# Memory stage in three token passes, with routing in short pieces, in a hybrid sparse/forgetting-attention and expert-retrieval step

## The chip, the cores and the metric

The kernel runs on one core of one Trainium2 chip. The metric is the time of one launch on the device in microseconds (us), the median of several runs. Engines: TensorE (PE), VectorE (DVE), ScalarE (ACT), GpSimd (POOL) and SyncE (SP), whose queue only issues DMA transfers. ScalarE and GpSimd can issue transfers too; the indirect ones (gathers of rows by index) are issued by GpSimd.

## The reference, cut to what matters

One layer over 1024 prompt tokens and 32 sample tokens, width 1024, in float32. After attention:

```python
h = x + concat([o_a, o_f]) @ w_out
h = h + memory_attention(rms_norm(h, g_mem), w_q, mk, mv, w_o)   # 4 heads of 256, 256 memory tokens
h = h + peer_ffn(rms_norm(h, g_ffn), ...)

def peer_ffn(xb):                       # per token, 8 heads
    q = xb @ w_q                        # 2048 wide: two halves of 128 per head
    s1, s2 = q[..., :half] @ keys1.T, q[..., half:] @ keys2.T      # 128 scores each
    v1, i1 = top_k(s1, 16); v2, i2 = top_k(s2, 16)
    sv, si = top_k(v1[:, None] + v2[None, :], 16)                  # of 256 pairs
    e = i1 * 128 + i2 at si             # expert numbers, of 16384
    return sum(softmax(sv) * gelu(xb . u[e]) * v[e])
```

## The kernel before, in words

Activations lie transposed: 128 partitions, 8 slices of the width (KD), tokens along the free axis. Tokens are in nine tiles: eight of 128 prompt tokens and one of the 32 sample tokens. Five of them (tiles 0 to 3 and the sample's, NSP = 544 tokens) are **gathered**: for each of their experts the rows of u and v are fetched by index. For 544 columns of indices that are 544 indirect transfers of 128 rows of 4 KB from u, each followed by one **dot** on VectorE (L1813, `dot`), a product with the token's own row, summed along 1024. Four prompt tiles (ND = 512 tokens) are **dense**: the hidden values of all 16384 experts are computed with matmuls (128 chunks of 128 experts, `DenseHidden`) and weighted later by spread gates.

A product in float32 precision is made of three fp32r products: weights and activations are each split in a high part (rounded) and a low part (the difference), and high x high, high x low and low x high are added. A **weight block** is 128 output rows by 1024: one load of 512 KB into one of two buffers `w`, a cast to the high part (L972) and a subtraction for the low part (L974), both on GpSimd (`split_w`), then 8 x 3 matmuls (L995, `product`) into one of three PSUM banks. `split_w` waits until the product two blocks back is done; a load waits for the split two blocks back.

A **pass** (`Mixer`) runs 40 blocks over its tokens: MIX 0 to 7 (output projection, added to h by `add_out`), a norm, QRY 8 to 15 (memory queries, `scale_q`), memory attention in units of one head and one token tile (`attend`, `attend_act`, `attend_dve`), ATT 16 to 23 (its output projection, added to h), a norm, PKQ 24 to 39 (the expert queries, copied by ScalarE, stored to the scratch tensor s_pq). Pass 1 is `sparse_mixer`: 544 tokens in two spans of 272 columns, so each block has 48 matmuls; 20 attention units; between MIX and QRY it also computes memory keys and values. It ends with a barrier, since it is a block of its own. Pass 2 is the first part of `route`: 512 tokens, 24 matmuls of 512 columns per block, 16 units.

**Routing** of one tile (its scores from s_pq and the keys on TensorE, then 20 ordered steps on VectorE: top-16 of each half by MAX8 and MATCH_REPLACE8, the 64 candidate pairs, top-16 again, the decoding of the positions by one-hot products of 2048 columns, L1970 to L1987) is written for VectorE as one list per tile, j = 0 to 8 in the order 0, 1, 2, 3, sample, 4 to 7. Between the ordered steps `beside` puts other work at fixed places: for j = 0 the adds of MIX (`OUT_AFTER`), for j = 1 the QRY scalings, the whole memory attention with three dots per unit, dots and the adds of ATT; for j >= 2 four dots after each of 16 steps. So pass 2 has tiles 0 and 1 in it by hand, and tile 2 begins after them. GpSimd issues the gathers in its own order between the splits, four row buffers up to dot 68 and twelve after it; a gather waits for the dot that last used its buffer.

**The hidden stage** is the second part of `route`: for chunk n ScalarE rounds the u block (L1472) and applies gelu to the product (L1495), GpSimd subtracts (L1477) and issues gathers (L1759), TensorE multiplies (L1487), SP loads and stores. The chunks are dealt to tiles by `CHUNKS_AT`; at the last chunk of group j ScalarE waits for tile j-1's scores to be sorted (`exponents(j - 1)`) before it goes on. After it come the gates (`spread_gates`) and the second half (`experts`).

## Time and profile before

| what | value |
|---|---|
| time, median of 3 runs (lowest to highest) | 4199.35 us (4198.51 to 4213.7) |
| the profiled execution: time, span | 4206.49 us, 4204.7 us |
| mean granted TensorE clock | 0.926 |
| busy: PE, DVE, ACT, POOL | 3559.5, 2489.5, 997.3, 2022.3 us |
| attention | 0 to 988 us |
| pass 1 | 988 to 1420 us |
| pass 2 | 1420 to 1887.8 us |
| hidden stage | 1887.8 to 2797 us |
| gates and second half | 2797 to 4204.7 us |

Times in a profile are counted from the span's start. The granted clock is a share of full speed: 1.00 is 2.4 GHz and 0.50 is 1.2 GHz, and a value between is a mean over a stretch that had both. The end of a matmul is modelled and successive ones overlap, so the pace is read from the starts. The bracket behind a timeline row is the idle time of the engine before it, and what ended that.

### The profile page before, as it was taken

Reading aid. Unit: us, or ns where it says so; the run is one execution under the profiler, and the core shown is the slowest. Engines: PE = TensorE matmul, PEld = TensorE weight load, DVE = VectorE, ACT = ScalarE, POOL = GpSimd, SP = SyncE. Lnnn points to the kernel's source line nnn. Section 1 sums busy time; section 2 is a strip of 40 time slices with the busy share of each in tenths; the row PEclk is TensorE's granted clock in tenths of the full one; section 3 lists DMA queues with packets and bytes.
Section 4 is the critical chain, followed back from the end, with each engine's and each line's share of the span. In section 5 each row is a group of like instructions: output and inputs, shape, how many; then the busy total and the mean of one; then the engine's idle time right before and its main releaser. Section 6 shows DMA issues by size and latency. Waiting matters only on the chain. (4 is left out here: it accounts for less than half of the span.)

```text
span 4204.7 us, 50892 instructions
## 1 busy us (share of the span) xinstructions
PE 3559.5 (85%) x17397; PEld 2546.1 (61%) x17413; DVE 2489.5 (59%) x5829; ACT 997.3 (24%) x1843; POOL 2022.3 (48%) x1518
## 2 busy tenths in 40 slices
PE   7888888897978874789898888957769999999996
PEld 4445566566768763567676666645535556566554
DVE  3878884332222375877999999998723333233333
ACT  1213333242121111113222222223212122122121
POOL 0000000003114443687888888855457677777762
PEclk9888998898999996899999999989979999999998
DMA  2011000003303435599999999969999999999983
GB/s 105 13 35 31 17 7 11 10 0 137 105 21 113 147 110 180 185 330 334 365 396 363 380 385 363 386 244 358 354 333 345 358 352 345 351 364 363 362 334 142
DMA packets 370010, 960.31 MB, mean 228 GB/s; under 512 B 33680, under 2 KB 119576, under 8 KB 368256
## 3 DMA queue, kind: packets, MB, share of 16 engines
q0 software_dynamic: 156672, 570.49, 35.7%
q1 hardware_dynamic: 205280, 363.30, 24.8%
q10 hardware_dynamic: 7840, 23.74, 1.5%
q8 instruction: 121, 1.98, 0.2%
q14 instruction: 97, 0.79, 0.1%
HBM read 862.73 MB, written 94.68 MB: 228 GB/s over the span
## 5 line engine op out<-in xcount | busy, mean ns | idle before, releaser
L1487 PE MATMUL m_ps<-m_xh,m_wh 128*128 128x512 f32 x3072 | 766.0, 407 | 100.1 <-POOL m_wh L1477 100.1
L2334 PE MATMUL e_y_ps<-e_wh,e_vh 128*128 128x512 f32 x3072 | 742.5, 398 | 51.0 <-DVE e_wh L2452 43.1
L1487 PEld LDWEIGHTS m_ps<-m_xh,m_wh 128*128 128x128 f32 x3072 | 585.2, 194 | 274.7 <-POOL m_wh L1477 142.3
L2334 PEld LDWEIGHTS e_y_ps<-e_wh,e_vh 128*128 128x128 f32 x3072 | 570.5, 189 | 269.7 <-issue 116.4
L972 POOL CAST m_wh<-m_w 128x1024 fp32r<-128x1024 f32 x80 | 84.6, 1057 | 1342.1 <-DMA m_w<-in_w_out 988.5
L995 PE MATMUL m_ps<-m_xh,m_wh 128*128 128x272 f32 (+1 forms) x2880 | 502.0, 335 | 65.6 <-DVE m_xh L1053 20.1
L995 PEld LDWEIGHTS m_ps<-m_xh,m_wh 128*128 128x128 f32 x2880 | 436.9, 194 | 127.4 <-issue 41.4
L2043 POOL DMA_INDIRECT e_rows<-in_v,idt x448 | 437.8, 977 | 119.7 <-issue 106.9
L2487 DVE TENSOR_TENSOR oT<-e_y_ps,oT 128x512 f32<-128x512 f32 x256 | 175.4, 685 | 520.6 <-PE e_y_ps L2334 520.6
L2412 POOL TENSOR_TENSOR e_vh<-e_v,e_vh 128x1024 fp32r<-128x1024 f32 x128 | 306.7, 2397 | 239.8 <-ACT e_vh L2357 238.5
L2076 PE MATMUL z_ps<-e_rows,flat 128*32 128x512 f32 x1792 | 291.5, 609 | 45.8 <-DMA e_rows<-in_v,idt 45.6
L1477 POOL TENSOR_TENSOR m_wh<-m_w,m_wh 128x1024 fp32r<-128x1024 f32 x128 | 313.1, 2446 | 13.8 <-ACT m_wh L1472 11.6
L1759 POOL DMA_INDIRECT oT<-in_u,eid x224 | 228.2, 1019 | 144.3 <-DVE hn L1813 108.0
L1813 DVE CUSTOM_DVE_ANT_0 oT<-oT,m_row_ps 128x1024 f32<-128x1024 f32 x224 | 262.6, 1212 | 29.5 <-DMA oT<-in_u,eid 28.5
L2365 ACT ACTIVATE e_wh<-e_hid 128x512 fp32r<-128x512 f32 x128 | 80.7, 632 | 746.0 <-DVE e_hid L2447 739.0
L2447 DVE TENSOR_TENSOR e_hid<-e_hid,e_gate 128x512 f32<-128x512 f32 x128 | 114.1, 892 | 208.9 <-DMA e_gate<-s_gate 208.9
L1495 ACT ACTIVATE flat<-m_ps 128x512 f32<-128x512 f32 x128 | 76.6, 598 | 597.0 <-PE m_ps L1487 596.9
L1813 DVE CUSTOM_DVE_ANT_0 m_q<-m_q,m_row_ps 128x1024 f32<-128x1024 f32 x160 | 188.0, 1211 | 33.6 <-DMA m_q<-in_u,eid 32.8
L974 POOL TENSOR_TENSOR m_wh<-m_w,m_wh 128x1024 fp32r<-128x1024 f32 x80 | 196.6, 2457 | 6.4
L1813 DVE CUSTOM_DVE_ANT_0 m_h<-m_h,m_row_ps 128x1024 f32<-128x1024 f32 x160 | 187.7, 1211 | 19.6 <-DMA m_h<-in_u,eid 18.5
L2140 PE MATMUL g_ps<-g_hot 128*128 128x128 f32 x1024 | 136.9, 289 | 64.5 <-DVE g_hot L2179 38.2
L2076 PEld LDWEIGHTS z_ps<-e_rows,flat 128*32 128x32 f32 x1792 | 57.8, 109 | 215.0 <-issue 108.3
(286 smaller groups left out, 5333.6 us busy)
## 6 DMA issues: line engine op xcount, KB each, us to landing
m_w<-in_ut SPq DMA_DIRECT2D x128, 512.0 KB, 5.4
e_v<-in_v SPq DMA_DIRECT2D x124, 512.0 KB, 7.2
s_hid<-flat SPq DMA_DIRECT2D x128, 256.0 KB, 6.8
e_hid<-s_hid SPq DMA_DIRECT2D x124, 256.0 KB, 7.3
e_gate<-s_gate SPq DMA_DIRECT2D x124, 256.0 KB, 6.5
s_gate<-g_stage SPq DMA_DIRECT2D x3, 8192.0 KB, 72.7
m_w<-in_w_pq SPq DMA_DIRECT2D x32, 512.0 KB, 3.8
m_w<-in_w_out SPq DMA_DIRECT2D x16, 512.0 KB, 3.9
```

The source lines that it names most:

```text
L974: pool.tensor_tensor(wh[:, at % 2, LO, :], w[:, at % 2, :], wh[:, at % 2, HI, :].bitcast(F32), ALU.subtract).then_inc(self.w_split, 1)
L995: mm = pe.matmul(self.bank(n, g), wh[:, at % 2, hw, k * P:(k + 1) * P], self.xh[:, hx, k, a:a + c], start=(k == 0 and o == 0), stop=(k == ...
L1477: pool.tensor_tensor(self.uh[:, at % 2, LO, :], self.u[:, at % 2], self.uh[:, at % 2, HI, :].bitcast(F32), ALU.subtract).then_inc(self.mx. ...
L1487: mm = pe.matmul(self.ps[:, i % 3, 0:ND], self.uh[:, at % 2, a, k * P:(k + 1) * P], self.xd[:, b, k, 0:ND], start=(k == 0 and o == 0), sto ...
L1759: pool.indirect_dma_start(out=rows[BUFFERS[d]], out_offset=None, in_=dram["u"], in_offset=bass.IndirectOffsetOnAxis(ap=eid[:, d:d + 1], ax ...
L1813: dve.tensor_tensor_reduce(out=row, in0=row, in1=row_flat, scale=1.0, scalar=0.0, op0=ALU.mult, op1=ALU.add, accum_out=hn[:, d:d + 1]).the ...
L2043: pool.indirect_dma_start(out=buffer, out_offset=None, in_=self.rows_dram, in_offset=bass.IndirectOffsetOnAxis(ap=self.idt[:, col:col + 1] ...
L2076: mm = pe.matmul(self.ps[g * 32:(g + 1) * 32, t % 2, half, :], self.wz[:, b // 4 % 2, b % 4 * P + g * 32:b % 4 * P + (g + 1) * 32], buffer ...
L2140: mm = pe.matmul(ps[:, q % 4, x, :], hot2[:, q % 4, x, :], hot1[:, q % 4, x, :], start=True, stop=True)
L2334: mm = pe.matmul(y_ps[:, o, 0:TD], vh[:, n % SLOT, a, m * P:(m + 1) * P], wh[:, SLOT - 1 - n % SLOT, b, g * TD:(g + 1) * TD], start=(c == ...
L2412: pool.tensor_tensor(vh[:, n % SLOT, LO, :], v[:, n % 2, :], vh[:, n % SLOT, HI, :].bitcast(F32), ALU.subtract).then_inc(v_split, 1)
L2487: dve.tensor_tensor(y[:, m, cols], y_ps[:, o % 4, 0:TD], y[:, m, cols], ALU.add).then_inc(y_added, 1)
```

## The change

The 1056 tokens go through the 40 blocks in three passes of 288, 256 and 512 tokens: W_A = tiles 0, 1 and the sample's 32, W_B = tiles 2 and 3, then the dense ones. The column order of the tokens follows (`pcols`, `order`). Spans disappear: each block is 24 matmuls over the whole width. `first_mixer` runs the 288 and keeps `split_w`; its end loads the keys already. `route` runs the two others, `mixers = (second, third)`; there the high part of a block is rounded by ScalarE (`high_w`) and GpSimd only subtracts (`low_w`), as for the chunks of the hidden stage. Each of the passes in `route` has its own x rows, ring of row buffers (four, four, six, then fourteen in the hidden stage) and limit of dots.

VectorE's routing and dots become one generator, `work`, which yields after each short piece with an estimate in us beside it (2.2 for eight MAX8, 1.3 for a dot, and so on). `Progress.fill(us)` runs pieces until the grant is used up. It is called before each block's add or scaling with 2.4 in the middle pass and 4.4 in the last one, also once per block of the expert queries, and with 1.3 at three places of each attention unit (after `normalize`, after `row_max`, after `split_result`). The decoding uses one one-hot array of 2048 columns instead of two, in 21 ordered steps. GpSimd's gathers follow marks of how many dots VectorE's list has reached three blocks before, plus 4 or 6. Tiles 0 and 1 are scored in the middle pass, 2 and 3 in the last; the hidden stage deals its chunks as 6, five times 23, and 7.

```diff
 NSP = C0 + T_S
+W_A = 2 * P + T_S
+W_B = NSP - W_A
...
-    if t < NS:
-        return slice(t * P, (t + 1) * P)
-    return slice(C0, NSP) if t == QT - 1 else slice(NSP + (t - NS) * P, NSP + (t - NS + 1) * P)
+    if t == QT - 1:
+        return slice(2 * P, 2 * P + T_S)
+    first = t * P + (T_S if t >= 2 else 0)
+    return slice(first, first + P)
 
 
...
+    def high_w(self, act, n):
+
+        at, w, wh = self.blocks_before + n, self.keep["w"], self.keep["wh"]
+        act.wait_ge(self.w_ready[at % 2], 16 * (at // 2 + 1))
+        act.wait_ge(self.bank_ready, at - 1)
+        act.activation(wh[:, at % 2, HI, :], w[:, at % 2, :], ACT.Copy).then_inc(self.w_high, 1)
+
+    def low_w(self, pool, n):
+
+        at, w, wh = self.blocks_before + n, self.keep["w"], self.keep["wh"]
+        pool.wait_ge(self.w_high, at - END + 1)
+        pool.tensor_tensor(wh[:, at % 2, LO, :], w[:, at % 2, :], wh[:, at % 2, HI, :].bitcast(F32),
+                           ALU.subtract).then_inc(self.w_split, 1)
+
...
-SPANS_S = ((0, 0, NSP // 2), (1, NSP // 2, NSP // 2))
-SPANS_D = ((0, 0, ND),)
 MIX, QRY, ATT, PKQ, END = 0, 8, 16, 24, 40
...
             self.normalize(dve, u)
+            if beside:
+                beside()
             if u + 2 < n:
                 self.row_max(dve, u + 2)
+            if beside:
+                beside()
             if u >= 1:
                 self.split_result(dve, u - 1)
             if beside:
-                beside(u)
+                beside()
...
-CHUNKS_AT = (0, 0, 0, 10, 19, 19, 19, 19, 19, 19, 4)
+CHUNKS_AT = (0, 0, 0, 0, 6, 23, 23, 23, 23, 23, 7)
...
-FEW, ALL = 4, 12
-WIDE_FROM = 68
-OUT_AFTER = {1: (0,), 2: (1,), 3: (2, 3), 5: (4,), 7: (5,), 15: (6,), 17: (7,)}
-QRY_AFTER = ((0,), (1,), (2, 3), (4, 5), (6,), (7,))
...
+class Progress:
+    def __init__(self, pieces):
+        self.pieces, self.owed, self.ended = pieces, 0.0, False
+    def one(self):
+        cost = next(self.pieces, None)
+        self.ended = cost is None
+        return cost or 0.0
+    def fill(self, us):
+        self.owed += us
+        while self.owed > 0 and not self.ended:
+            self.owed -= self.one()
+    def until(self, reached):
+        while not reached() and not self.ended:
+            self.one()
...
+        RINGS = ([12, 13, 8, 9], [12, 13, 4, 5], list(range(6)), list(range(14)))
...
+            def work():
+                for j in range(QT):
+                    yield from slot(j)
+                tail(QT - 1)
+                yield 2.6
+                yield from dots(N_DOT)
+            progress = Progress(work())
+            def reach(j, q):
+                progress.until(lambda: n_step[0] >= STEPS * j + q)
+            def mark():
+                marks.append((n_dot[0], n_eid[0]))
+            for i, mx in enumerate(mixers):
+                norm_q, norm_f = norms[i]
+                us = (2.4, 4.4)[i]
+                for k in range(KD):
+                    mx.split_src(dve, k)
+                dve.wait_ge(h_loaded, 32 + 16 * i)
+                for n in range(MIX, QRY):
+                    progress.fill(us)
+                    mx.add_out(dve, n)
+                    mark()
+                if i == 1:
+                    reach(1, TAIL)
+                for k in range(KD):
+                    mx.split_gained(dve, k)
+                norm_q.dve(dve)
+                dve.wait_ge(norm_q.normed, norm_q.all)
+                for n in range(QRY, ATT):
+                    progress.fill(us)
+                    mx.scale_q(dve, n)
+                    mark()
+                if i == 0:
+                    reach(0, S_DONE)
+                mx.attend_dve(dve, lambda: progress.fill(1.3))
+                if i == 0:
+                    reach(0, TAIL)
+                else:
+                    reach(2, S_DONE)
+                attended.append((n_dot[0], n_eid[0]))
+                for n in range(ATT, PKQ):
+                    progress.fill(us)
+                    mx.add_out(dve, n)
+                    mark()
+                if i == 1:
+                    reach(2, TAIL)
+                norm_f.dve(dve)
+                dve.wait_ge(norm_f.normed, norm_f.all)
+                mx.make_x(dve)
+                for n in range(PKQ, END):
+                    if i == 0 and n == PKQ + 11:
+                        first_dots.append(n_dot[0])
+                        now[0] = RINGS[1]
+                    progress.fill(us)
+                    mark()
+                if i == 0:
+                    reach(1, S_DONE)
+                first_dots.append(n_dot[0])
+                now[0] = RINGS[i + 2]
+            progress.until(lambda: False)
+            assert n_step[0] == STEPS * QT
...
+                def ordered(op, cost):
+                    op.then_inc(step, 1)
+                    n_step[0] += 1
+                    done[0] += 1
+                    yield cost
+                    if j >= 1:
+                        yield from dots(DOTS_TO[j] + DOTS_AT[j] * min(done[0], 16) // 16)
+                    dve.wait_ge(step, STEPS * j + done[0])
...
+                dve.wait_ge(s_copied, 2 * j + 2)
+                for c in range(16):
+                    op = dve.max(half(v, c)[:, 0:8], st[:, c])
+                    if c % 8 == 7 and c < 15:
+                        yield 2.2
+                yield from ordered(op, 2.2)
+                for c in range(16):
+                    op = dve.match_replace(rep[0:M, c], half(v, c)[:, 0:8], st[:, c], TAKEN)
+                    if c % 8 == 7 and c < 15:
+                        yield 2.8
+                yield from ordered(op, 2.8)
+                for c in range(16):
+                    dve.max(half(v, c)[:, 8:16], rep[0:M, c])
+                    op = dve.max_index(half(iu, c)[:, 0:8], half(v, c)[:, 0:8], st[:, c])
+                    if c % 4 == 3 and c < 15:
+                        yield 2.6
+                yield from ordered(op, 2.6)
...
+            def next_high(i, n):
+                if n < END:
+                    mixers[i].high_w(act, n)
+                elif i == 0:
+                    mc.high_w(act, n - END)
+                else:
+                    hidden.round(act, n - END)
...
+                    if n == CHUNKS_TO[4]:
+                        show_rows(1)
...
+            def beside(i, mark):
+                n_dots, n_eids = mark
+                gathers(min(n_dots + (4, 6)[i], P * n_eids, first_dots[i + 1]))
+            for i, mx in enumerate(mixers):
+                for n in range(END):
+                    mx.low_w(pool, n)
+                    if n >= 3:
+                        beside(i, marks[i * END + n - 3])
+                    if i == 1 and n == 1:
+                        gathers(first_dots[1] + 6)
+                    if n == ATT + 1:
+                        beside(i, attended[i])
+                    if n == PKQ + 1:
+                        for k in range(1, KD, 2):
+                            mx.split_x(pool, k)
+                gathers(first_dots[i + 1])
...
+                    last = min(DOTS_TO[j] + 10, N_DOT)
+                    gathers(first + -(-(last - first) * (i + 1) // CHUNKS_AT[j]))
...
+                first = mixer(0, W_A, [(0, P, 0), (P, P, 0), (2 * P, T_S, 1)], keep["oA"], keep["oA"], None)
+                second = mixer(W_A, W_B, [(0, P, 0), (P, P, 0)], keep["oB"], keep["oB"], first)
+                third = mixer(NSP, ND, [(t * P, P, 0) for t in range(ND // P)], keep["oD"], None, second)
+                first_mixer(nc, dram, keep, (first, second), sems)
...
-    order = np.concatenate([np.arange(C0), np.arange(T_P, NT), np.arange(C0, T_P)])
+    order = np.concatenate([np.arange(2 * P), np.arange(T_P, NT), np.arange(2 * P, T_P)])
```

## Rows read from the trace of the kernel before

**Rows 1.** Windows by stage: busy us (instructions) of PE, PEld, DVE, ACT, POOL; clock, DMA, GB/s.

```profile
988.00:1420.00 432.00, 382.01 (x2591) 345.15 (x2591) 92.08 (x181) 73.65 (x170) 144.25 (x84) 0.96 0.27 91
1420.00:1562.00 142.00, 110.23 (x469) 87.05 (x468) 109.26 (x412) 20.85 (x36) 67.06 (x39) 0.89 0.38 124
1562.00:1699.00 137.00, 61.52 (x224) 51.73 (x223) 74.81 (x160) 19.92 (x64) 46.55 (x49) 0.61 0.54 177
1699.00:1887.80 188.80, 159.40 (x627) 120.17 (x627) 155.21 (x414) 25.69 (x42) 147.77 (x108) 0.92 0.75 261
1887.80:2797.00 909.20, 787.36 (x3288) 610.11 (x3288) 851.56 (x2227) 240.31 (x314) 752.88 (x563) 0.96 0.98 369
```

**Rows 2.** Timeline of PE, pass 1 and the entry to pass 2: start, us.

```profile
1020.15 6.39 PE L995 MATMUL m_ps<-m_xh,m_wh 128*128 128x272 f32 x48
...
1027.10 6.39 PE L995 MATMUL m_ps<-m_xh,m_wh 128*128 128x272 f32 x48
...
1304.46 1.02 PE L995 MATMUL m_ps<-m_xh,m_wh 128*128 128x272 f32 x3 [10.06 <-DVE m_xh L1053]
...
1435.97 3.78 PE L1617 MATMUL m_a_ps<-r_keys,r_pqt 128*128 128x128 f32 x16 [15.55 <-DMA r_keys<-in_keys]
```

**Rows 3.** Timeline of POOL, first two blocks of pass 1.

```profile
988.95 1.04 POOL L972 CAST m_wh<-m_w 128x1024 fp32r<-128x1024 f32 x1 [988.50 <-DMA m_w<-in_w_out]
...
992.36 1.04 POOL L972 CAST m_wh<-m_w 128x1024 fp32r<-128x1024 f32 x1
```

**Rows 4.** DMA issues of pass 1: count, KB each, median us to landing.

```profile
m_w<-in_w_pq SPq DMA_DIRECT2D x16, 512.0 KB, 3.5
```

**Rows 5.** Timeline of PE, pass 2.

```profile
1444.36 17.48 PE L995 MATMUL m_ps<-m_xh,m_wh 128*128 128x512 f32 x72
...
1510.88 7.13 PE L995 MATMUL m_ps<-m_xh,m_wh 128*128 128x512 f32 x24 [12.47 <-DVE m_xh L1021]
...
1531.42 11.39 PE L995 MATMUL m_ps<-m_xh,m_wh 128*128 128x512 f32 x48 [0.55 <-DVE m_q L1036]
...
1774.36 6.78 PE L995 MATMUL m_ps<-m_xh,m_wh 128*128 128x512 f32 x15 [9.36 <-DVE m_xh L1053]
...
1802.56 19.15 PE L995 MATMUL m_ps<-m_xh,m_wh 128*128 128x512 f32 x72 [5.89 <-POOL m_wh L974]
...
1887.85 12.47 PE L1487 MATMUL m_ps<-m_xh,m_wh 128*128 128x512 f32 x52 [1.03 <-POOL m_wh L1477]
```

**Rows 6.** Timeline of DVE: two attention units of pass 1, then of pass 2.

```profile
1180.20 0.42 DVE L1172 TENSOR_REDUCE m_nmax<-m_ps 128x1 f32<-128x256 f32 x1 [1.40 <-PE m_ps L1084]
...
1183.78 0.42 DVE L1172 TENSOR_REDUCE m_nmax<-m_ps 128x1 f32<-128x256 f32 x1 [1.40 <-PE m_ps L1084]
...
1572.92 0.42 DVE L1172 TENSOR_REDUCE m_nmax<-m_ps 128x1 f32<-128x256 f32 x1 [2.49 <-PE m_ps L1084]
...
1581.84 0.42 DVE L1172 TENSOR_REDUCE m_nmax<-m_ps 128x1 f32<-128x256 f32 x1 [2.49 <-PE m_ps L1084]
1583.96 0.42 DVE L1165 TENSOR_TENSOR m_xh<-m_a_ps,m_xh 128x256 fp32r<-128x256 f32 x1 [1.70 <-ACT m_xh L1149]
```

**Rows 7.** Timeline of POOL, two gathers in a row.

```profile
1790.61 0.94 POOL L1759 DMA_INDIRECT m_h<-in_u,eid  x1 [0.30 <-issue]
1791.86 0.94 POOL L1759 DMA_INDIRECT m_h<-in_u,eid  x1 [0.30 <-issue]
```

**Rows 8.** Hidden stage: windows of L1813, L1759, L1477; then groups of DVE.

```profile
1887.80:2797.00 909.20, 514.90 (x876) 0.96 0.98 369
1887.80:2797.00 909.20, 442.06 (x435) 0.96 0.98 369
1887.80:2797.00 909.20, 310.69 (x127) 0.96 0.98 369
...
L1979 DVE TENSOR_TENSOR oT<-oT,r_fi 128x2048 f32<-128x2048 f32 x12 | 31.3, 2647 | 0.2
```

**Rows 9.** Window in the attention of pass 1; columns as in the first group.

```profile
1164.00:1214.00 50.00, 30.37 (x191) 25.71 (x189) 18.04 (x57) 17.78 (x58) 1.61 (x1) 1.00 0.03 11
```

856 lines of the change are left out of this document (428 added, 428 removed).

## The prediction

> **What bounds the kernel now.** I read the granted clock and the busy slices first, then one table by stage [rows 1]; the reader is to see which engine is full in each. Attention runs to 988 us and isn't touched. Pass 1 (544 tokens, to 1420) is TensorE: 382 of 432 us busy, VectorE 92, GpSimd 144. Pass 2 (512 dense tokens, to 1887.8) carries tiles 0, 1 and most of 2 and 106 dots; in its attention (1562 to 1699) nothing is full and the clock is at 0.61. The hidden stage (1887.8 to 2797) has VectorE at 852 of 909 us and the DMA at 0.98. The second half (gates, experts: 1408 us) gets the same inputs in another column order and stays.
>
> The hidden stage has a second full engine. A gather is listed with 0.94 us, but successive ones start 1.25 us apart [rows 7]. 435 of them and 127 subtractions of 310.7 us [rows 8] are 435 x 1.25 + 311 + 6 of small gaps = 861 us of GpSimd in 909. So VectorE and GpSimd bound it together; the PE needs only 128 x 5.7 plus scores, about 750. Moving work off VectorE alone would help little; what counts is how many gathers AND dots are out of it.
>
> **What the schedule of the change moves.** I add up the estimates that the diff writes beside its pieces. Tile 0 has 60.3 us of them, each later one 62.9 and, for tiles 1 and 2, 64 dots x 1.3 = 83.2. The middle pass grants 40 x 2.4 + 8 x 3 x 1.3 = 127.2, the last 40 x 4.4 + 16 x 3 x 1.3 = 238.4: 365.6 in all. Tiles 0 to 2 take 60.3 + 2 x 146.1 = 352.5, and 13 us reach two ordered steps of tile 3. So (adding piece by piece in the written order) 132 dots are done at the start of the hidden stage (25 after the middle pass), against 106: 438 dots are there now (876 entries, two each) [rows 8]. Now tile 2 also still owes its multiplications (12 full-height L1979, the pairs of six tiles, beside the sample's) [rows 8], some 17 us, and tile 3 all of it.
>
> **The first pass, 544 to 288 tokens.** Two spans of 272 are 48 matmuls in 6.39 us, so about 6.1 per block, 6.94 with the norm's sums [rows 2]. At 0.127 us for 272 columns (6.1 / 48) and 0.234 for 512 (11.39 / 48, [rows 5]) a matmul of 288 takes 0.133, a block 3.2 us. GpSimd needs more: cast plus subtraction repeat after 3.41 [rows 3], and the weights land in 3.5 us [rows 4] in one of two buffers, (3.5 + 3.5 + 0.2) / 2 = 3.6 per block. I take 3.6: 40 x (6.1 - 3.6) = 100 us saved. The norm's sums (16 x 0.85) and two of five row transposes (together with the rest of them under GpSimd's pace: 8) vanish under it: 22. Attention is 12 units for 20 at 3.58 [rows 6]: 29. Shorter norms and first blocks (a wait of 10.06 stands in it [rows 2]): 11. Total 162: pass 1 ends at 1258. The memory keys and values (62 us, PE) stay.
>
> **A middle pass is added (256 tokens).** Entry: scores now wait 15.55 for the keys after the barrier [rows 2], and products begin 24 after pass 1; keys are there already after the change, s_pq (1 MB) is not: 21. A block is 24 x 0.119 = 2.9 us of PE. ScalarE rounds (1.05) and GpSimd subtracts (2.45): the weights' loop is (3.5 + 1.05 + 2.45 + 0.3) / 2 = 3.65, GpSimd with one gather 2.45 + 1.25 + 0.1 = 3.8. VectorE has 2.4 granted, in fact about 2.0 (a tile's 63 are about 53: 851.6 - 514.9 = 336.7 for six tiles and the 17 us), plus 0.42. So: mix 28, norm 3, queries 28, scores 5, attention 61, output 28, norm and first block 11, peer queries 15 x 3.95 + 3 = 62. Sum 226. Bounds for a block: 2.9 (PE) and 5.7 (half clock). The pass issues 40 more loads of 512 KB on SP's queue, 21 MB, where the DMA is 27 to 54% busy [rows 1]; the stores of its queries wait there behind one load each, as now. Two queues get new neighbours. On GpSimd a gather that waits for a dot holds the next subtraction, and so the PE; the first one waits for tile 0's ids, in the middle pass's attention, and that gather's landing (a few us) is not in the sum. On VectorE the add that frees a bank stands behind the piece before it (at most 2.8 us), which three banks cover.
>
> Attention with pieces: a unit is 3.58 alone and 8.92 with three dots in one place, at the low clock; of that 8.92, VectorE idles 2.49 and 1.70 [rows 6]. The change puts one piece of 1.3 on average into each idle place and one in the open. I take 0.5 + 2.49 + 0.42 + 1.70 + 0.42 + 1.2, and 0.4 for pieces of 2.3 to 2.8 that outgrow the 1.70: 7.1 us. Bounds: 3.58 + 1.2 = 4.8 and 8.92. Eight units are 57, with first and last 61.
>
> **The last pass (512).** Start 2 (no barrier), mix 8 x 6.15 with scores and a wait for s_pq 56, norm 3 (now 12.47, because the tile's last steps stand before it [rows 5]), queries 48, attention 16 x 7.1 = 114 (now 137), output 55.5, norm and first block 20.5 (9.36 idle, as now [rows 5]), peer queries 15 x 5.9 = 88 (now 102: a wait of 5.89 and several of 1.3 for the split weights [rows 5], since GpSimd casts, subtracts and issues 2.5 gathers; the cast goes to ScalarE). Late rows in rings of six, gathers held three blocks behind: 7. Sum 394, against 443.5 from 1444.4 to 1887.8 [rows 5].
>
> The hidden stage starts at 1258 + 21 + 226 + 394 = 1899, 11 us later than now.
>
> **The hidden stage.** 412 gathers x 1.25 + 128 x 2.5 = 835 on GpSimd, against 861. VectorE: 851.6 less 26 dots x 1.18 = 31, tile 2's 17 and tile 3's first 10 is 794. ScalarE shows the rows of tile 1 only after the first chunk, so VectorE starts some 12 us late, GpSimd's first free gather 10 us late. The PE also stalls: only six chunks precede the wait of ScalarE for tile 3's exponents, near 80 to 100 us in; it still has 121 x 5.72 + 17 = 709 to go, less than GpSimd's 728, so this hides. Now 909 is 861 plus 48 of waits and tail; then 835 + 10 + 8 tail + 15 (the 23 chunks per tile need 23 x 2.5 + 64 x 1.25 = 137.5 of GpSimd and 127.5 of VectorE, so one engine leads where two were level) = 868. That gains 41. Bounds: 850 and 909. Here also the copy into tile pieces, W_A and the column order cost nothing by themselves.
>
> Sum: +11 - 41 = -30. The profiled execution has span 4204.7 and time 4206.49; so 4174.7 in its span. It stands 7 us above the median of 4199.35, from which 30 taken gives **4169**.
>
> **A rule that speaks against it.** In the attention of pass 1 the PE is 61% busy and the clock stays 1.00 [rows 9]; at 8.92 us per unit it is 0.61 [rows 1]. The Trainium skill, TensorE: Matmul & The Clock Gate, section "HAM oscillation — how this bites in real kernels", says that thin products with waits between them fall back to the low clock again and again. By that rule every block of the two narrow passes would run at 1.2 GHz. The sum above takes the high clock, from rows of this case.
>
> **Rivals.**
> 1. The clock falls in the narrow passes. There the PE waits 0.4 of 3.6 us, and 0.8 of 3.65, per block. At the low clock a block of 256 is 5.7 us, 2.1 more, one of 288 6.4, 2.8 more. 25 of the 80 blocks lose the 53 us that turn -30 into slower; the middle pass alone gives 4169 + 84 = 4253. For it: 0.61 at attention, which stands between blocks. Against: 1.00 with the PE 61% busy [rows 9]. 0.14; with rows that come late in rings of four as the source of the PE's waits, the same place and price, 0.22.
> 2. The hidden stage gains nothing: the stall of PE and ScalarE at six chunks, with the split of chunk 7 behind 60 gathers, moves GpSimd's load back, and it stays 905. 4206. 0.22.
> 3. The pieces vanish in attention's idle places and the clock stays up: 24 units at 5.2, -45; hidden 858, -10: 4114. 0.16.
> 4. The change as forecast, 4140 to 4195: 0.40; about 0.30 of it below 4178.
>
> **Chances and range.** A measurement of this kernel can tell 0.5%, 21 us, from no change. Faster: 0.30 + 0.16 + a little of 2 = 0.48. Slower: 0.22 + 0.02. Same: 0.28. Range: down to rival 3, 4112, and up past rival 2 into the mild part of rival 1, 4228.
>
> **What would show it.** First products of the middle pass near 1279, of the last near 1505, the hidden stage near 1899; blocks 3.6 apart in pass 1 and 3.65 to 4 in the middle one, clock over 0.9 in both; attention units near 7; 412 dots in the hidden stage of 868 us, GpSimd 95% full with gathers 1.25 apart; a PE hole after chunk 6. It is wrong if the narrow blocks take 5 us or more, if VectorE waits for gathered rows inside the passes, or if the hidden stage waits for ScalarE.

## The result and the profile after

The changed kernel takes 4226.92 us (median, 4219.8 to 4233.82) beside 4202.21 us of the kernel before in the same runs: ratio 1.0057, 95% interval 1.0043 to 1.007. It is slower by 25 us; the forecast was 4169 us, faster. The profiled execution has a span of 4231.9 us, 27.2 more than before. Executions of one kernel of this family spread by some 12 us to either side, and single stages do so too: over the runs below that leave it as it is, the middle pass takes 248.4 to 258.3 us, the last pass 386.0 to 388.1 and the hidden stage 898.5 to 908.4. A difference of one stage between two single profiles counts only above that, or where the wait that makes it is seen.

The windows of the changed kernel (busy us and instructions of PE, PEld, DVE, ACT, POOL; granted clock, DMA share, GB/s): pass 1, the middle pass without its end, the last pass, the hidden stage. They answer to [rows 1].

```profile
988.00:1272.00 284.00, 244.71 (x1448) 207.72 (x1448) 60.79 (x114) 45.08 (x113) 137.62 (x83) 0.93 0.37 121
1290.00:1530.00 240.00, 174.29 (x1170) 161.04 (x1169) 138.04 (x534) 75.57 (x132) 120.15 (x68) 0.85 0.51 168
1540.00:1926.00 386.00, 308.59 (x1287) 243.86 (x1288) 265.65 (x610) 100.51 (x173) 210.26 (x150) 0.87 0.63 219
1926.00:2829.00 903.00, 766.57 (x3254) 612.27 (x3252) 807.29 (x2158) 234.99 (x307) 734.16 (x543) 0.93 0.96 357
```

No engine is full in the middle and the last pass. The time is in the waits, and the timeline of PE has them at the seams (they answer to [rows 2, 5]):

```profile
1283.22 3.75 PE L1923 MATMUL m_a_ps<-m_keys,r_pqt 128*128 128x128 f32 x16 [11.76 <-DMA r_pqt<-s_pq]
...
1524.64 5.25 PE L998 MATMUL m_ps<-m_xh_flat,m_wh 128*128 128x256 f32 x24 [7.91 <-POOL m_wh L979]
1539.84 12.70 PE L998 MATMUL m_ps<-m_xh_flat,m_wh 128*128 128x512 f32 x48 [9.95 <-DVE m_xh_flat L1009]
...
1606.06 8.19 PE L998 MATMUL m_ps<-m_xh_flat,m_wh 128*128 128x512 f32 x24 [8.37 <-DVE m_xh_flat L1023]
...
1666.72 3.78 PE L1081 MATMUL m_ps<-m_mk_p,m_q_flat 128*128 128x256 f32 x8 [10.59 <-DVE m_q_flat L1035]
...
1829.19 4.44 PE L998 MATMUL m_ps<-m_xh_flat,m_wh 128*128 128x512 f32 x9 [9.36 <-DVE m_xh_flat L1051]
...
1925.87 16.80 PE L1502 MATMUL m_ps<-m_xh_flat,m_wh 128*128 128x512 f32 x72
1954.07 8.30 PE L1502 MATMUL m_ps<-m_xh_flat,m_wh 128*128 128x512 f32 x24 [11.40 <-POOL m_wh L1492]
```

The table gives each stretch from its first product to the first product of the next one, in us. The hidden stage runs to the first matmul of the gates, at 2829.31, and 2800.13 before.

| stretch | before | predicted | after |
|---|---|---|---|
| pass 1 ends | 1420 | 1258 | 1271.4 |
| entry (end of pass 1 to the next product) | 24 | 21 | 18.5 |
| middle pass with the join | – | 226 + 2 | 249.9 |
| last pass | 443.5 | 392 | 386.0 |
| hidden stage begins | 1887.85 | 1899 | 1925.87 |
| hidden stage | 912.3 | 41 less | 903.4 |

The passes cost 38 us more than before instead of 11, and the hidden stage gives back 9 instead of 41; with 2 us less in the second half that is the 27 us of the spans. So the profile stands 57 us above the forecast of -30: 32 of them in the hidden stage, 22 in the middle pass and 13 in pass 1, while the entry, the last pass and the second half took 10 less than forecast.

### The profile page after: what moved, and what is told of

It is laid out like the page before. It is cut to its first block and busy times, and to the rows that moved or that the text cites. A ratio compares the mean times of both kernels' runs of the same rounds, so it can differ in the third digit from the quotient of the medians.

```text
span 4231.9 us, 51219 instructions
## 1 busy us (share of the span) xinstructions
PE 3563.6 (84%) x17413; PEld 2564.6 (61%) x17413; DVE 2479.0 (59%) x5857; ACT 1082.2 (26%) x1964; POOL 2070.4 (49%) x1522
## 5 line engine op out<-in xcount | busy, mean ns | idle before, releaser
L1502 PE MATMUL m_ps<-m_xh_flat,m_wh 128*128 128x512 f32 x3072 | 748.4, 404 | 120.7 <-POOL m_wh L1492 120.7
L1502 PEld LDWEIGHTS m_ps<-m_xh_flat,m_wh 128*128 128x128 f32 x3072 | 591.8, 195 | 272.4 <-POOL m_wh L1492 147.4
L998 PE MATMUL m_ps<-m_xh_flat,m_wh 128*128 128x288 f32 (+2 forms) x2880 | 515.6, 338 | 93.7 <-POOL m_wh L979 29.2
L963 POOL CAST m_wh<-m_w 128x1024 fp32r<-128x1024 f32 x40 | 42.1, 1051 | 1116.7 <-DMA m_w<-in_w_out 986.6
L998 PEld LDWEIGHTS m_ps<-m_xh_flat,m_wh 128*128 128x128 f32 x2880 | 446.0, 198 | 159.9 <-issue 52.0
L2221 POOL DMA_INDIRECT e_rows<-in_v,idt x448 | 435.5, 972 | 119.8 <-issue 107.9
L1624 DVE CUSTOM_DVE_ANT_0 oT<-oT,m_row_ps 128x1024 f32<-128x1024 f32 x289 | 343.4, 1215 | 127.9 <-DMA oT<-in_u,eid 109.6
L2141 POOL DMA_INDIRECT oT<-in_u,eid x289 | 298.3, 1032 | 165.4 <-DVE hn L1624 96.6
L1624 DVE CUSTOM_DVE_ANT_0 m_q_flat<-m_q_flat,m_row_ps 128x1024 f32<-128x1024 f32 x129 | 152.8, 1214 | 57.0 <-DMA m_q_flat<-in_u,eid 56.6
L2318 PEld LDWEIGHTS g_ps<-g_hot 128*128 128x128 f32 x1024 | 124.5, 198 | 81.3 <-DVE g_hot L2357 44.7
```

What stands on the lines that cost most here:

```text
L998: mm = pe.matmul(self.bank(n), wh[:, at % 2, hw, k * P:(k + 1) * P], self.xh[:, hx, k, :], start=(k == 0 and o == 0), stop=(k == KD - 1 an ...
L1502: mm = pe.matmul(self.ps[:, at % 3, 0:ND], self.uh[:, at % 2, a, k * P:(k + 1) * P], self.xd[:, b, k, :], start=(k == 0 and o == 0), stop= ...
L1624: dve.tensor_tensor_reduce(out=rows[b], in0=rows[b], in1=row_flat, scale=1.0, scalar=0.0, op0=ALU.mult, op1=ALU.add, accum_out=hn[:, d:d + ...
L2141: pool.indirect_dma_start(out=rows[b], out_offset=None, in_=dram["u"], in_offset=bass.IndirectOffsetOnAxis(ap=eid[:, d:d + 1], axis=0)).th ...
L2221: pool.indirect_dma_start(out=buffer, out_offset=None, in_=self.rows_dram, in_offset=bass.IndirectOffsetOnAxis(ap=self.idt[:, col:col + 1] ...
L2318: mm = pe.matmul(ps[:, q % 4, x, :], hot2[:, q % 4, x, :], hot1[:, q % 4, x, :], start=True, stop=True)
```

## The experiments

All times of stages below are from one profile each, bounded as in the table. A ratio is to the kernel before in the same runs; times of two experiments are compared by their ratios where their runs differ.

**e1. Another deal of the hidden chunks.**

```
-CHUNKS_AT = (0, 0, 0, 0, 6, 23, 23, 23, 23, 23, 7)
+CHUNKS_AT = (0, 0, 0, 0, 16, 21, 21, 21, 21, 21, 7)
```

> The changed kernel with the 128 hidden-stage chunks dealt 16, 21, 21, 21, 21, 21, 7 over the routing slots in place of 6, 23, 23, 23, 23, 23, 7; nothing else. Theory A (the deal starves TensorE: in the first group 70 gathers are issued between 6 weight splits, 12 to a split, and TensorE idled 58 us there in 7 waits on the split, while the later groups are then too long for the DMA engines): the stage loses 15 to 30 us, total 4227 -> 4197 to 4212. Theory B (the stage is set by the bytes of the whole stage at the rate of the DMA engines, or by VectorE's dots, wherever the chunks lie): no change, 4222 to 4232. Theory C (the short first group is what lets VectorE run ahead, with more chunks in it the scores of the fourth slot come late): slower by 5 to 15 us.

4207.49 us, ratio 1.0006 (0.9991 to 1.0021); the hidden stage took 886.4 us, 17 less. Theory A. VectorE's waits for gathered rows in the stage fell from 83 to 50 us.

**e2. The last stores of the middle pass, earlier on SyncE's queue.**

```
-                        for m in range(END - 3, END):
-                            mb.store_pq(sp, m)
...
                 for n in range(2, 27):
                     mx.load(sp, n)
+                    if i == 1 and n == 2:
+                        mb.store_pq(sp, END - 1)
...
                     mc.load(sp, 0)
+                    mb.store_pq(sp, END - 3)
                     mc.load(sp, 1)
+                    mb.store_pq(sp, END - 2)
```

> The changed kernel with the last three query stores of the middle pass issued one behind each of the first weight loads of the last pass on SyncE's queue, in place of all three behind the fourth load. Theory A (at the join ScalarE's copy waits 7.02 us for a store that stands behind those loads, and its rounding of the next operand and TensorE's first product are queued behind the copy): the wait of 9.95 us at the join falls to about 3, the total by 5 to 7 us. Theory B (the store is held up by the 2048 KB reload of the residual on the same queue, not by the order): the wait moves by less than 1 us and the total stays.

The wait at the join fell from 9.95 to 4.46 us, and middle pass with join took 241.3 us instead of 249.9, as A says. But the last pass took 391.3 us and the total didn't move: 4234.22, ratio 1.0064 (1.0046 to 1.0083). The cause of the 9.95 us is shown; that removing it alone pays is not.

**e3, e4. The hidden rows hardly stored, in both kernels.**

```
+ w = ND if n == 0 else 16
- sp.dma_start(dram["s_hid"][n], hid[:, e % 2, 0:ND])
+ sp.dma_start(dram["s_hid"][n][:, 0:w], hid[:, e % 2, 0:w])
- eng.dma_start(hid[:, n % 2, :], dram["s_hid"][n])
+ eng.dma_start(hid[:, n % 2, :], dram["s_hid"][0])
```

> The changed kernel, but of the hidden rows only the first chunk is stored whole, of the other 127 only 16 of 512 columns; the second half loads the first chunk's rows each time, so the rest of the work is as before and the output is not the reference's. The stage then moves 33 of its 322 MB less. Theory A (the DMA engines' rate bounds the stage: they were busy 0.97 to 1.01 of its steady part): the stage of 898 us falls by 45 to 85 us. Theory B (POOL's 412 gathers at 1.25 us and 128 splits at 2.5 us bound it, as the prediction took it): falls by under 10 us. Theory C (VectorE: dots and routing, 803 us busy): under 15 us.

> The kernel before with the same leaving out of the hidden stores as the run beside it; the output is not the reference's. Theory A (DMA rate bounds its hidden stage too: busy share 0.97 to 1.03): the stage of 909 us falls by 40 us or more. Theory C (VectorE, 854 us busy of 913, bounds it): it falls by under 20 us. Theory B (POOL): under 10 us.

One time each: 4220.21 and 4200.78 us. The hidden stage took 903.5 us (903.4 with the stores) and 906.8 (912.3). Theory A is out: a DMA share of 0.96 to 1.0 in the windows didn't mean that bytes set the time.

**e5. The second token row copied before the first chunk.** e1, and

```
+ show_rows(1)                      # ahead of the loop over the chunks
- if n == CHUNKS_TO[4]: show_rows(1)    # was behind the first gelu
```

> The kernel with 16 chunks in the first group (e1) and, besides, ScalarE's copy of the second token row ahead of the hidden stage instead of behind the first chunk's gelu, which waits for TensorE's first product. Theory A (the stage is VectorE's: it was busy 818 of 886 us there, waited 50 us for gathered rows and 17.0 us once for this copy): the 17.0 us wait falls below 5 us, the stage from 886 to 870 to 876, the total by 10 to 17 us against e1. Theory B (the stage is paced by TensorE and the splits, VectorE has slack): the wait goes, the stage stays within 3 us of 886.

4216.42 us, ratio 1.0015 (0.9996 to 1.0034): the total can't be told from e1. VectorE's wait for the copy fell only to 10.4 us, not below 5: the copy now stands behind the last queries' copies. The hidden stage took 875.3 us, 11 less than e1, and GpSimd's wait for ScalarE in it 13.5 us instead of 26.8. But e8 and e14 below have e1's hidden stage with the copy where it was, and took 877.3 and 877.9 us with 19.4 and 18.7 us of that wait; e6, e9 and e10, with the copy moved, took 874.9, 875.6 and 880.1. So a gain by the copy is not shown: most of what e1's profile has more than e5's it has more than those of e8 and e14 too.

**e6. The residual reloaded later.** e5 and e2, and

```
-                    if i == 0 and n == END - 2:
-                        sp.wait_ge(h_stored, 32)
-                        sp.wait_ge(dotted, first_dots[0])
-                        sp.wait_ge(mx.x_scaled, 16)
-                        sp.dma_start(mc.h, dram["xP"][...]).then_inc(h_loaded, 16)
...
                     mc.load(sp, 1)
                     mb.store_pq(sp, END - 2)
+                    (the five lines above, without the if)
```

> e5 and besides the three stores of e2 and the 2048 KB reload of the residual moved behind the first two weight loads of the last pass on SyncE's queue. Theory A (the reload is what held up the weight of the middle pass's last product: ScalarE waited 11.2 us for it and TensorE 7.91): that wait falls below 2 us, the join stays near 3 us, the middle pass ends 6 to 8 us earlier, and the hidden stage starts 8 to 15 us earlier than in e5. Theory B (routing and dots on VectorE set the end of the last pass too: what TensorE saves at the join comes back as waits for VectorE in the last pass, as e2 showed with 391 us for it instead of 386): the last pass grows by what is saved and the hidden stage starts within 4 us of e5's start.

4193.21 us, ratio 0.9979 (0.9962 to 0.9996). The 7.91 us wait is gone, the middle pass with the join took 234.2 us (249.9 in the changed kernel), the last pass 392.9 us (388.1 in e5). So A holds for the seam, and about 5 us of it comes back in the last pass as B said.

**e7. The 128 dots of the passes over 8 of 1024 columns.**

```
+ w = slice(0, 8) if d < P else slice(0, D)
- dve.tensor_tensor_reduce(out=rows[b], in0=rows[b], in1=row_flat, ...
+ dve.tensor_tensor_reduce(out=rows[b][:, w], in0=rows[b][:, w], in1=row_flat[:, w], ...
```

> The changed kernel with the 128 dots that lie in the passes taken over 8 of 1024 columns; the gathers stay whole and the output is not the reference's. VectorE's work in the middle and the last pass falls by about 128 x 1.15 = 147 us of the 404 us that it was busy. Theory A (the dots lie in VectorE's idle time and what hurts is late rows, which it still waits for): hidden stage starts at 1920 to 1930 as before. Theory B (dots delay the operations that TensorE waits for): it starts 15 to 40 us earlier than 1925.9. The hidden stage itself stays 903 us either way.

One time, 4228.19 us; the hidden stage began at 1919.3, most of the 6.6 us before it started (pass 1 and the entry), and middle and last pass took 249.3 and 384.6 us. Theory A: while rows come at the same times, shorter dots give the passes 2 us at most. What VectorE saved it spent waiting for rows. The view of VectorE's waits in the last pass, first of the changed kernel and then of e7 (us in all, times, longest):

```profile
DVE oT L1624 <- DMA oT<-in_u,eid: 68.0, 39, 7.7
```

```profile
DVE oT L1625 <- DMA oT<-in_u,eid: 138.7, 59, 10.6
```

**e8. Rows asked for one block earlier.** e1, and

```
- if n >= 3: beside(i, marks[i * END + n - 3])
+ if n >= 2: beside(i, marks[i * END + n - 2])
```

> e1 with GpSimd allowed one block further ahead with its gathers in the two last passes (the mark of two blocks back instead of three). Theory A (rows come late because they are asked for late: VectorE waited 41 us for rows in the middle pass and 68 us in the last, and its next operation for TensorE stood behind): those waits fall by half or more and the hidden stage starts 5 to 15 us earlier than in e1 (1924.0). Theory B (GpSimd then waits for VectorE's dots ahead of the next weight split, and TensorE for the split): waits of TensorE for the split grow and the stage starts later by 5 to 20 us.

4198.82 us, ratio 0.9983 (0.9968 to 0.9998), some 10 us under e1, where the two intervals still overlap. The waits for rows in the last pass fell from 67.5 to 30.4 us and it took 378.5 us instead of 387.6; the middle pass stayed (250.1 against 252.0). In the last pass TensorE's wait for VectorE ahead of the attention fell from the changed kernel's 10.59 to 3.15 us, the one at the norm from 8.37 to 3.42, and its waits for splits rose from 4.4 to 9.5. The timeline of PE in e8:

```profile
1598.63 7.29 PE L998 MATMUL m_ps<-m_xh_flat,m_wh 128*128 128x512 f32 x24 [3.42 <-DVE m_xh_flat L1023]
...
1655.40 2.45 PE L1081 MATMUL m_ps<-m_mk_p,m_q_flat 128*128 128x256 f32 x8 [3.15 <-DVE m_q_flat L1035]
```

Here the dots are whole, so late rows are shown to have made most of those two waits.

**e9. All four edits (e1, e5, e6, e8) together.**

> All four edits together: the chunks of e1, the early row of e5, the stores and the reload of e6, the gathers one block further ahead of e8. Theory A (the stalls are separate, each gives what it gave alone): against e6 (4193) the last pass falls from 393 to about 382 and the total to 4178 to 4188, faster than the kernel before by 0.4 to 0.7%. Theory B (what e8 saved in the last pass, 9 us, and what e6 saved at the join, 15 us, is the same slack of VectorE): total 4190 to 4196.

4184.61 us, ratio 0.9967 (0.9951 to 0.9982): middle pass with join 235.8, last pass 386.3, hidden stage 875.6. Theory A by the total. The seam's gain stays, and the last pass is 7 us shorter than e6's; e10, whose passes are the same as here, took 377.7 us for it. So the earlier rows do give something on top of the seam, somewhere between 7 and 15 us.

**e10. e9 with a longer lead of the gathers in the hidden stage.**

```
- last = min(DOTS_TO[j] + 10, N_DOT)
+ last = min(DOTS_TO[j] + 14, N_DOT)
```

> e9 with the gathers of the hidden stage running 14 rows ahead of the slot's dots instead of 10 (there are 14 row buffers). Theory A (rows are asked for late there too: VectorE waited 50 us for rows in e1's hidden stage of 886): the waits for rows halve and the stage gives another 10 to 20 us. Theory B (the ring is full when VectorE pauses for routing, GpSimd waits for a free buffer ahead of the next split, so a longer lead cannot be used): within 4 us of e9, or slower by up to 8 with TensorE waiting for the splits.

4186.73 us, ratio 0.9957 (0.9943 to 0.9971), hidden stage 880.1. No difference from e9: theory B.

**e11. One part of the change alone, on the kernel before: its three dots of an attention unit in three places.**

```
  self.normalize(dve, u)
+ beside(u, 1)
  self.row_max(dve, u + 2)
+ beside(u, 2)
  self.split_result(dve, u - 1)
- beside(u)       # dots(3 * (u + 1))
+ beside(u, 3)    # dots(3 * u + place)
```

> The kernel before with one part of the change alone: in the attention of its second pass the three dots of a unit stand one at each of three places instead of all three behind the unit. Theory A (short pieces between the operations are what shortened the units, 8.92 us before): the 16 units take 110 to 125 us instead of 143, the total falls by 10 to 25 us to 4180 to 4195. Theory B (the same three dots delay the same chain wherever they stand): units stay at 8.5 us or more, total within 5 us.

4159.05 us, ratio 0.9893 (0.9878 to 0.9907): 45 us faster than the kernel before and, by the ratios, 69 faster than the change. Theory A, and beyond its range: the second pass took 401.9 us instead of 443.5, the hidden stage 911.2. The timeline of VectorE, two units:

```profile
1600.28 0.43 DVE L1172 TENSOR_REDUCE m_nmax<-m_ps 128x1 f32<-128x256 f32 x1 [1.24 <-PE m_ps L1084]
1600.62 1.21 DVE L1817 CUSTOM_DVE_ANT_0 oT<-oT,m_row_ps 128x1024 f32<-128x1024 f32 x1
1601.75 0.08 DVE L1817 DVE_READ_ACCUMULATOR2_ANT hn<- 128x1 f32 x1
1602.26 0.42 DVE L1165 TENSOR_TENSOR m_xh<-m_a_ps,m_xh 128x256 fp32r<-128x256 f32 x1 [0.43 <-ACT m_xh L1149]
1602.60 1.21 DVE L1817 CUSTOM_DVE_ANT_0 oT<-oT,m_row_ps 128x1024 f32<-128x1024 f32 x1
...
1604.20 1.21 DVE L1817 CUSTOM_DVE_ANT_0 oT<-oT,m_row_ps 128x1024 f32<-128x1024 f32 x1
1605.34 0.08 DVE L1817 DVE_READ_ACCUMULATOR2_ANT hn<- 128x1 f32 x1
1606.25 0.42 DVE L1172 TENSOR_REDUCE m_nmax<-m_ps 128x1 f32<-128x256 f32 x1 [0.82 <-PE m_ps L1084]
```

In [rows 6] the maximum waited 2.49 us and the subtraction 1.70. Here two of the unit's three dots lie in those waits, which are down to 1.24 (0.82) and 0.43, and the maxima are 5.97 us apart, not 8.92. Over the 16 units the mean distance of the transposes is 5.95 us; it was 8.50.

**e12. No rows in the passes.**

```
+ if d < P: a dot over 4 numbers already in SBUF and PSUM, no wait for a row   (VectorE)
+ if d < P: return                                                             (GpSimd's gather)
```

> The changed kernel without the gathers of the first 128 rows and with their dots taken over 4 numbers at hand; the output is not the reference's. The hidden stage keeps its 412 rows. Theory A (rows that come late are what holds VectorE's next operation, and TensorE behind it, in the two last passes: 50 and 68 us of waits, and in e7 they only grew when the dots were short): the hidden stage starts 20 to 45 us earlier than 1925.9. Theory B (the passes are paced by the splits, the norms and the attention alone, and rows and dots hide): it starts within 8 us of 1925.9.

One time, 4188.15 us. Theory A: the hidden stage began at 1883.2 us, 43 earlier; middle pass with join 235.8 us (14 less), last pass 355.0 (31 less), hidden stage 898.5. The run takes away the rows, their issue on GpSimd and the dots' 1.2 us each at once, so the 45 us are the price of all three together.

**e13. Short dots in the hidden stage.**

```
+ w = slice(0, 8) if d >= P else slice(0, D)    # as in e7
```

> The changed kernel with the dots of the hidden stage (all but the first 128) taken over 8 of 1024 columns; gathers, splits and stores stay whole and the output is not the reference's. VectorE's work there falls by 416 x 1.15 = 478 us. Theory A (VectorE's work and its waits bound most of the stage): the stage of 903 us falls to 780 to 850 us. Theory B (GpSimd: 412 x 1.25 + 128 x 2.5 = 835 us of it, and its waits for others): it stays above 870 us.

One time, 4219.40 us. VectorE's busy time in the stage fell from 807 to 386 us, and the stage only from 903.4 to 885.4. Theory B as far as VectorE is concerned: its dots don't set the stage. That GpSimd sets it is not tested by this run; none took work off GpSimd alone.

**e14. The attention's pieces in one place.** e1, and

```
- beside() at three places of the unit, progress.fill(1.3) each
+ beside() at the last of them,         progress.fill(3.9)
```

> e1 with the pieces of the attention in one place behind each unit, 3.9 us granted at once instead of 1.3 us at each of three places; beside e1. Theory A (the three places are what makes a unit 5.7 us: undone, VectorE's next operation of the unit waits behind 3.9 us or more): the units go back to 7.5 to 9 us, 24 units cost 45 to 75 us more than in e1. Theory B (the units are short because the routing pieces are shorter than the dots, wherever they stand): units stay under 6.5 us, the total within 10 us of e1.

4263.05 us, ratio 1.0146 (1.0132 to 1.0161), 56 us more than e1: theory A. The middle and the last pass took 267.1 and 429.4 us, 57 more than in e1 together. The distance of the transposes was 7.69 us in the middle pass and 8.09 in the last; in e1 it was 5.70 and 5.64. Its timeline of VectorE shows the two waits of [rows 6] again:

```profile
1713.47 0.42 DVE L1162 TENSOR_TENSOR m_xh_flat<-m_a_ps,m_xh_flat 128x256 fp32r<-128x256 f32 x1 [1.58 <-ACT m_xh_flat L1146]
...
1719.13 0.42 DVE L1169 TENSOR_REDUCE m_nmax<-m_ps 128x1 f32<-128x256 f32 x1 [2.49 <-PE m_ps L1081]
```

**e15, e16. e11 with two other deals of the chunks.**

```
- CHUNKS_AT = (0, 0, 0, 10, 19, 19, 19, 19, 19, 19, 4)
+ CHUNKS_AT = (0, 0, 0, 16, 18, 18, 18, 18, 18, 18, 4)    # e15
+ CHUNKS_AT = (0, 0, 0, 6, 20, 20, 20, 20, 20, 18, 4)     # e16
```

> e11 (the kernel before with its dots in three places) and besides the deal of the chunks 16, 18, 18, 18, 18, 18, 18, 4 instead of 10, 19, 19, 19, 19, 19, 19, 4. Theory A (a slot of 18 chunks leaves TensorE and VectorE more even, rows come less late): the hidden stage falls from 911 to 895 to 905, total 4159 to 4145 to 4155. Theory B (VectorE is busy 855 of 911 there, so the deal moves nothing): within 4 us of e11.

> e11 with the chunks of the hidden stage dealt 6, 20, 20, 20, 20, 20, 18, 4 instead of 10, 19, 19, 19, 19, 19, 19, 4: more rows between two splits in the first group. Theory A (VectorE sets the later groups there, and what it loses in the first one is not made good, as in e15): it is busier in the first 100 us, the stage falls from 911 to 895 to 908. Theory B (GpSimd sets it: the splits wait behind 11 gathers each and TensorE idles in the first group as in the changed kernel): the stage grows by 5 to 20 us.

4196.79 us (0.9982, 0.9969 to 0.9996) and 4167.91 (0.9914, 0.9884 to 0.9944); hidden stages 947.5 and 924.2 us, both longer than e11's 911.2. Neither theory of e15 foresaw a loss. Of e16's two the stage speaks for B, but its profile is the slowest of its four executions (4180 us) and its ratio can't be told from e11's. The windows of e15's hidden stage, its first 102 us and two later stretches of 120:

```profile
1838.00:1940.00 102.00, 101.17 (x452) 81.53 (x451) 59.73 (x82) 34.57 (x45) 72.34 (x45) 1.00 0.81 282
...
2300.00:2420.00 120.00, 102.03 (x419) 78.93 (x419) 119.76 (x331) 29.97 (x41) 96.89 (x74) 0.94 0.97 362
2420.00:2540.00 120.00, 99.02 (x407) 76.45 (x408) 119.76 (x328) 29.63 (x39) 95.89 (x74) 0.94 0.98 366
```

With 16 chunks in the first group its gathers are spread over TensorE's 16 products; VectorE is busy 59.7 of 102 us there (82.0 in e11), and in the two later stretches it is full (119.8 of 120). Over the whole stage, though, VectorE idles 55 us in both kernels (947.5 - 891.9, 911.2 - 856.2): what it idles more at the start it idles less later. What grew by the stage's 36 us is its busy time, for the same operations; the last section shows how they are stretched. A like deal (16 chunks first) gained 17 us in the three-pass kernel, where VectorE has 47 us less to do in the stage.

## Why the prediction was wrong

**Which steps failed.** Two carry most of the 57 us: in the hidden stage "+ 10 + 8 tail + 15" for the waits (32 us), and in the middle pass waits that the sum put at nothing, for the first gathered rows and on SyncE's queue (22 us). The third, the price of late rows in the last pass, was also too low, but attention gave back as much there.

**Late rows.** "Late rows in rings of six, gathers held three blocks behind: 7", and for the middle pass that the first gather's landing "is not in the sum". e12 puts a price on rows, gathers and dots of the passes together: 45 us, 14 in the middle and 31 in the last. e7 shows that shorter dots alone give 2 us at most, and e8 that asking earlier takes 37 of 67.5 us of VectorE's waits and 9 us of the last pass. How much of the 31 us would stay with rows at hand and whole dots was not run. The text named this as what would make it wrong ("if VectorE waits for gathered rows inside the passes") but priced it at 0.08, as a source of rival 1's waits. A wait of VectorE costs so much here because it stands in the program ahead of the operation that TensorE needs. The 10.59 us before the attention of the last pass are such a case: TensorE's last query product ended near 1656, and the timeline of VectorE has the scaling of its result (L1035) behind dots and three pieces of routing:

```profile
1657.89 1.22 DVE L1624 CUSTOM_DVE_ANT_0 oT<-oT,m_row_ps 128x1024 f32<-128x1024 f32 x1 [0.21 <-DMA oT<-in_u,eid]
...
1659.64 3.91 DVE L1767 TENSOR_TENSOR oT<-oT,r_fi 128x2048 f32<-128x2048 f32 x1
1663.47 0.28 DVE L1775 TENSOR_TENSOR r_sab<-r_place,r_start 128x128 f32<-128x128 f32 x1
1663.78 2.29 DVE L1778 TENSOR_REDUCE r_num<-oT 128x128 f32<-128x2048 f32 x1
1665.99 0.68 DVE L1035 SCALAR_TENSOR_TENSOR m_q_flat<-m_ps,flat 128x512 f32<-128x512 f32 x1
```

In e12 this wait is 2.9 us, and the one at the norm 3.4 instead of 8.4; e8 has 3.15 and 3.42 with whole dots. GpSimd's issue of the gathers is not the price in the last pass: TensorE waited only 4.4 us for splits there. In the middle pass it may be part of the 14: TensorE's waits for splits there are 24.9 us, and 17.7 in e12. A run with gathers but no waits for them wasn't tried.

**The middle pass, 226 + 2, measured 249.9.** Besides the rows, the mis-sized step is SyncE's queue: "the stores of its queries wait there behind one load each, as now". At this seam three of them stood behind four loads, and the 2048 KB reload of the residual, which the sum has no term for, went ahead of the last weight block. The timeline of ScalarE in the changed kernel shows both:

```profile
1521.11 1.06 ACT L973 ACTIVATE m_wh<-m_w 128x1024 fp32r<-128x1024 f32 x1 [11.22 <-DMA m_w<-in_w_pq]
...
1538.07 0.38 ACT L1061 ACTIVATE flat<-m_ps 128x256 f32<-128x256 f32 x1 [7.02 <-DMA s_pq<-flat]
1538.35 4.26 ACT L1004 ACTIVATE m_xh_flat<-oT 128x512 fp32r<-128x512 f32 x8
```

The rounding of the last pass's operand stands behind a copy that waits for a store. e2 and e6 took both away, 16 us. With the 14 of e12 that is 30 us, and shorter attention units gave some 11 back. The prediction named the queue, but gave its stores no cost and left the reload out.

**Pass 1, predicted to end at 1258, ended at 1271.5.** A product of 288 columns took 3.46 us, not the 3.2 interpolated from 272 and 512 (where the text has 0.234 us for 512 columns, 11.39 / 48 is 0.237), so a block with the norm's sums is 3.67 and these sums don't vanish under GpSimd's pace. The excess over 3.6 per block sits in two places: the eight MIX blocks took 39.0 us instead of 28.8, with a wait of 5.03 for ScalarE's first square and a block of 5.61 behind it, and the sixteen of the expert queries 65.6 instead of 57.6. Other terms gave 5 of these 18 us back.

**Attention, predicted 7.1 us per unit, measured 5.7.** The mechanism was right (e14 undoes it: 7.7 to 8.1), the gain forecast too small by 1.4 x 24 = 34 us. The sum put a unit's two waits in full and a third piece in a row; in e11's rows the waits with a dot in them are down to 1.24 and 0.43. This is where the last pass made good what it lost in waits: 386 for a predicted 392, with 10.59 before attention and 8.37 instead of 3 at the norm.

**The hidden stage, predicted 41 us shorter, was 9 shorter.** That VectorE's dots don't set it is shown: with VectorE's work halved (e13) it moves by 18 us. That GpSimd does fits the rows but is argued. GpSimd's own time holds up: 412 gathers and 128 splits at the sum's rates are 835 us, and before 861. What failed is "+ 10 + 8 tail + 15", 33 us for all the rest. It is 903 - 835 = 68 us; before it was 912 - 861 = 51, and the change was to bring it down. In the trace's own count, where a gather that waits for a dot has no gap at issue, GpSimd is busy 734.5 us with 84.8 of gaps at issue and waits 84 (before: 755.6, 77.9 and 79). The wait that grew is that for ScalarE's rounding. GpSimd's waits in the stage, in the changed kernel:

```profile
POOL m_wh L1492 <- ACT m_wh L1487: 36.1, 21, 8.9
...
POOL oT L2141 <- DVE hn L1624: 18.1, 29, 6.7
POOL m_h_flat L2141 <- DVE hn L1624: 11.8, 24, 2.5
...
POOL m_q_flat L2141 <- DVE hn L1624: 7.0, 18, 2.4
```

The wait for ScalarE was 10.7 us before, the waits for VectorE 57.4. With 16 chunks in the first group the first is down, to 26.8 us in e1, 19.4 in e8 and 18.7 in e14; in e5 it is 13.5:

```profile
POOL m_wh L1492 <- ACT m_wh L1487: 13.5, 5, 5.0
...
POOL oT L2140 <- DVE hn L1624: 11.7, 32, 2.2
POOL m_h_flat L2140 <- DVE hn L1624: 10.1, 19, 3.7
...
POOL m_q_flat L2140 <- DVE hn L1624: 6.7, 16, 2.2
```

So the deal of the chunks accounts for 17 to 26 of the missing 32 us (886.4, 877.3 and 877.9 us in e1, e8 and e14, for 903.4). What the copy of the second row adds is not told from the scatter (875.3, 874.9, 875.6 and 880.1 with it moved), and the rest stays open. The hole after chunk 6 that rival 2 named is there behind the third chunk already: TensorE waited 11.40, 8.35, 9.68, 8.89, 9.11 and 9.52 us for splits between 1954 and 2044, with some twelve gathers between two splits. The prediction had seen this stall and let it hide behind GpSimd's total. It doesn't: with the stall gone (e1, 1.5 to 4.2 us per wait there) the stage is shorter by 17 us or more, though GpSimd has the same work.

**The rivals.** Rival 1, the clock, came in small pieces only. It is 1.00 from 1225 to 1265 (288 columns) and from 1415 to 1441 (256 columns), low in attention (0.67 from 1360 to 1408, and 0.50 then 0.84 in the last pass), and 0.89 from 1410 to 1530: three blocks of the narrow pass there took 4.58, 4.35 and 5.25 us for 3.13, behind waits of 2.36, 2.79 and 7.91 us. That is some 5 us, not 84. The prediction also stretched the rule that it set against itself: the section of the Trainium skill that it names (TensorE: Matmul & The Clock Gate, "HAM oscillation — how this bites in real kernels") has waits longer than the products between them; here the usual wait per narrow block is 0.4 to 0.8 us beside products of 3.1 to 3.5, and the clock stays up. Rival 2 (the stage stays, stall in the six-chunk group) is what happened there, with the waits in the passes on top. Rival 3's attention came true (5.7 for its 5.2), and was outweighed.

**What the change as a whole trades.** e11 and e9 both have short pieces in the attention of route, and e9 has its seams in order. They differ in the number of passes and in what came with it: rounding on ScalarE, the rings and marks of the gathers, the decoding, the deal of the chunks. From the first product to the hidden stage e11 takes 851.4 us and e9 918.8: three passes and the rest cost 67. The hidden stage takes 911.2 and 875.6: it gives 36 back. The medians of the same runs, 4159.05 and 4184.61, are 26 us apart. The kernel to keep is e11.

## What to carry to other kernels

A part of a change that only moves pieces into idle places should be tried without the rest: here it was worth 45 us alone, and what stood around it cost more than it gave. When a wait for data (a gathered row, a store's completion) is placed in an engine's program, price what stands behind it in that program, not the wait as a share of the engine's idle time. An engine that is 90% full has two terms, its work and its waits, and a smaller work term helps only as far as the waits for its neighbours don't grow. Before a few us of one stage are credited to an edit, look for other runs that have this stage unchanged: here they took away the 11 us that e5 alone seemed to show.
